# Keys projected from gain-scaled tokens first, their shift added afterwards, and one query projection taken last in the head of a diffusion-transformer block

## The chip, the core and the metric

The kernel runs on one core of one Trainium2 chip. The metric is the device time of one execution in microseconds (us). TensorE (PE) multiplies; ScalarE (ACT) and VectorE (DVE) read its sums from PSUM, convert weights and scale tokens; GpSimd (POOL) and SyncE (SP) issue transfers, ACT some too. Every engine runs its own instructions strictly in order and waits on semaphores.

## What is computed

One block of a diffusion transformer on 256 latent and 256 context tokens of width 2048. Only its beginning matters here:

```python
mod = jax.nn.silu(c) @ ada_w[i] + ada_b[i]                 # (1, 6 * 2048)
sh1, sc1, g1, sh2, sc2, g2 = jnp.split(mod[:, None, :], 6, axis=-1)
mod_c = jax.nn.silu(c_ctx) @ ada_w[i] + ada_b[i]           # the same weights, for the context
h  = rms_norm(x,   norm1_g[i]) * (1 + sc1)  + sh1          # modulate
hc = rms_norm(ctx, norm1_g[i]) * (1 + csc1) + csh1
proj = h @ w_in[i]                                         # q, k, v of two branches, gates
... hc @ w_in[i][:, :N_QKV]                                # q, k, v of the context
```

Two attention branches, their merge, an output projection and a gated MLP with a convolution follow.

## The kernel before

**Number format.** A float32 weight is split into a rounded part w_hi and a remainder w_lo, activations likewise (hT, part 0 and part 1), and a product is hi·hi + hi·lo + lo·hi. A weight unit is 128 x 1024 numbers (two channel groups of 128 by 512 columns, 512 KB). ACT casts it to w_hi, DVE subtracts to w_lo, four such pairs of slots exist (SPLIT_SLOTS), and `raw` has eight landing slots (SLOTS).

**The head.** The 2048 channels are 16 groups `kc`, in four quarters `q`. The modulation product silu(c) @ ada_w for shift and scale is made on PE from raw float32: one `unit_ada(q, kc)` is four matmuls of 32 weight columns over 256 columns each (the profile has eight records for them), reads one 512 KB unit that holds shift and scale columns side by side, and 16 of them finish shift and gain of a quarter. Then a chain runs through three engines: ACT copies the sums (`read_mod_rows`), PE transposes them (`turn_mod`), DVE adds the bias and makes gain and shift (`modulation1`), ACT multiplies the transposed tokens by gain and adds shift (`modulate`, from `turn_tokens` on PE), DVE splits them into hT (`split_modulated`).

**Keys inside the head.** The first job, the keys' projection (job 0), runs between those units: `head_k(s, t)` makes six matmuls for weight unit s (channel groups 2s, 2s+1) and column tile t, once both groups of hT are ready. The table K_TILES says behind which `unit_ada` each of the 32 tiles stands. Job 1 (queries, `projection(1)`) and job 2 (values) follow.

**Other queues.** SP issues all weight loads in the order of HEAD. ACT issues the small parameter loads and the two 2 MB token loads. POOL loads the other columns of ada_w into `ada_raw`, which the keys' weights used until then; DVE sums those in `ada_steps` from job 1 on, by the table ADA_STEPS. From job 1 on each job is a dense run of matmuls with weights two to eight units ahead.

## Time and profile before

| | us |
|---|---|
| median of 3 runs (1720.74 to 1722.42) | 1720.74 |
| the profiled execution | 1720.02 |
| its span, first to last instruction | 1718.3 |
| PE busy / ACT busy / DVE busy in the span | 1677.8 / 752.6 / 1086.3 |
| key tiles start | 52.13 |
| query job (job 1) starts | 131.87 |
| value job (job 2) starts | 154.06 |

A busy PE is not PE at its peak: matmuls overlap in the records, so of a run of them the distance from start to start counts. PEclk is the clock that PE was granted, as a share of 2.4 GHz: 1.00 is 2.4 GHz, 0.50 is 1.2 GHz, and values between are a stretch with both. The chain that ended last is followed back from the last instruction.

### The profile page before, as it was taken

To read this page: it belongs to the slowest core of one execution; us is meant where nothing else is said; L and a number is where in the kernel's file an instruction comes from. 1 tells how busy PE (TensorE), PEld (TensorE's weight loads), DVE (VectorE), ACT (ScalarE), POOL (GpSimd) and SP (SyncE) were. 2 spreads that over 40 slices of the span, in tenths; PEclk is the share of its full clock that TensorE was granted. 3 is DMA by queue.
4 is the path that set the end of the run, shared out by engine and by line. 5 is a ranking of instruction groups with operands and counts; after the bars stand their busy time and mean duration, and the time that the engine had idled before them with its cause. 6 is when DMAs were issued, how large, how long until landed. Compare 5 with 4: busy or idle time off the path is not lost.

```text
span 1718.3 us, 23725 instructions
## 1 busy us (share of the span) xinstructions
PE 1677.8 (98%) x8768; PEld 1371.5 (80%) x8768; DVE 1086.3 (63%) x1366; ACT 752.6 (44%) x962; POOL 108.6 (6%) x161
## 2 busy tenths in 40 slices
PE   4999999999999999999999999999999999999997
PEld 1568888888888678888888788888888888888886
DVE  1338787768887674554555666666666666655556
ACT  2233321623222664444444555555555555544444
POOL 0002222122121000000000000000000000000000
PEclk7999999999999999999999999999999999999999
DMA  9999888269896128566565566666666665655552
GB/s 353 386 387 347 298 296 297 79 215 328 259 321 200 52 90 271 191 189 191 192 234 195 148 190 190 188 191 188 191 187 191 185 184 188 202 195 194 191 193 83
DMA packets 161813, 371.47 MB, mean 216 GB/s; under 512 B 11671, under 2 KB 12423, under 8 KB 160598
## 3 DMA queue, kind: packets, MB, share of 16 engines
q1 hardware_dynamic: 140240, 291.65, 52.5%
q0 software_dynamic: 20144, 74.22, 12.7%
q10 hardware_dynamic: 1366, 4.74, 0.7%
q8 instruction: 41, 0.67, 0.2%
q14 instruction: 22, 0.18, 0.0%
HBM read 368.36 MB, written 2.21 MB: 216 GB/s over the span
## 4 chain that ended last, share of the span: by engine, by line
PE 94%; DMA 3%; DVE 1%; issue 0%; ACT 0%; SPq 0%; DVEq 0%; POOL 0%; ACTq 0%
PE ps L1885 21%; PE ps L1884 11%; PE ps L1899 10%; PE ps L1901 10%; PE ps L1900 10%; PE ps L2253 5%; PE ps L2252 5%; PE ps L2254 5%; PE ps L1811 4%; PE ps L1813 3%; PE ps L1812 3%; DMA raw<-in_ada_w 3%; PE ps L1882 1%; PE ps L1803 1%; PE ps L1968 1%; PE ps L1950 1%
## 5 line engine op out<-in xcount | busy, mean ns | idle before, releaser
L1147 DVE TENSOR_TENSOR w_lo<-raw,w_hi 128x1024 fp32r<-128x1024 f32 x480 | 584.5, 1223 | 419.7 <-ACT w_hi L680 419.2
L680 ACT CAST w_hi<-raw 128x1024 fp32r<-128x1024 f32 x480 | 503.4, 1050 | 763.3 <-PE ps L1885 271.2
L1885 PE MATMUL ps<-h2T,w_hi 128*128 128x512 f32 x1320 | 462.7, 394 | 0.0
L1884 PE MATMUL ps<-h2T,w_lo 128*128 128x256 f32 x1320 | 366.8, 278 | 0.0
L1885 PEld LDWEIGHTS ps<-h2T,w_hi 128*128 128x128 f32 x1320 | 247.8, 188 | 53.7
L1884 PEld LDWEIGHTS ps<-h2T,w_lo 128*128 128x128 f32 x1320 | 248.2, 188 | 3.9
L1899 PE MATMUL ps<-w_hi,hT 128*128 128x512 f32 x512 | 201.7, 394 | 0.0
L1901 PE MATMUL ps<-w_hi,hT 128*128 128x512 f32 x512 | 199.4, 389 | 0.0
L1900 PE MATMUL ps<-w_lo,hT 128*128 128x512 f32 x512 | 199.3, 389 | 0.0
L1222 DVE SCALAR_TENSOR_TENSOR ada_acc<-ada_raw,silu_c,ada_acc 128x512 f32<-128x512 f32 x240 | 179.9, 750 | 29.4 <-DMA ada_raw<-in_ada_w 14.1
L603 POOL DMA_DIRECT2D ada_raw<-in_ada_w x128 | 91.2, 712 | 381.5 <-DVE ada_acc L1222 226.4
L1899 PEld LDWEIGHTS ps<-w_hi,hT 128*128 128x128 f32 x512 | 96.1, 188 | 21.2 <-issue 1.9
L1901 PEld LDWEIGHTS ps<-w_hi,hT 128*128 128x128 f32 x512 | 96.1, 188 | 20.3
L2252 PE MATMUL ps<-w_hi,f_hi 128*128 128x512 f32 x288 | 112.0, 389 | 0.0
L2253 PE MATMUL ps<-w_lo,f_hi 128*128 128x512 f32 x288 | 112.0, 389 | 0.0
L2254 PE MATMUL ps<-w_hi,f_lo 128*128 128x512 f32 x288 | 112.0, 389 | 0.0
L1900 PEld LDWEIGHTS ps<-w_lo,hT 128*128 128x128 f32 x512 | 96.2, 188 | 19.1
L1811 PE MATMUL ps<-hT,w_hi 128*128 128x512 f32 x256 | 103.9, 406 | 1.0 <-DVE hT L1205 1.0
L1813 PE MATMUL ps<-hT,w_lo 128*128 128x512 f32 x256 | 100.0, 390 | 0.0
L1812 PE MATMUL ps<-hT,w_hi 128*128 128x512 f32 x256 | 99.9, 390 | 0.0
L1885 PE MATMUL ps<-hT,w_hi 128*128 128x512 f32 x240 | 84.2, 393 | 0.0
L1884 PE MATMUL ps<-hT,w_lo 128*128 128x256 f32 x240 | 67.3, 280 | 0.0
(231 smaller groups left out, 1985.6 us busy)
## 6 DMA issues: line engine op xcount, KB each, us to landing
raw<-in_ffn_w_up SPq DMA_DIRECT2D x176, 512.0 KB, 3.8
raw<-in_w_in SPq DMA_DIRECT2D x152, 512.0 KB, 4.8
ada_raw<-in_ada_w POOLq DMA_DIRECT2D x128, 512.0 KB, 5.9
raw<-in_ffn_w_down SPq DMA_DIRECT2D x88, 512.0 KB, 4.3
raw<-in_ada_w SPq DMA_DIRECT2D x64, 512.0 KB, 10.4
raw<-in_w_out SPq DMA_DIRECT2D x32, 512.0 KB, 4.4
raw<-in_w_branch_a SPq DMA_DIRECT2D x16, 512.0 KB, 3.6
raw<-in_w_branch_b SPq DMA_DIRECT2D x16, 512.0 KB, 3.6
```

The costliest lines, as they stand in the source:

```text
L680: act.copy(w_hi[:, s % SPLIT_SLOTS, :], raw[:, s, :]).then_inc(hi_ready[s], 1)
L1147: dve.tensor_tensor(w_lo[:, s % SPLIT_SLOTS, :], raw[:, s, :], w_hi[:, s % SPLIT_SLOTS, :], ALU.subtract).then_inc(lo_ready[s], 1)
L1222: dve.scalar_tensor_tensor(acc, raw_columns, silu_c[:, kc:kc + 1], acc, ALU.mult, ALU.add).then_inc(ada_summed, 1)
L1811: pe.matmul(o, w_hi[:, row4(slot), at], hT[:, :, 0, kc, :], start=(kc == 0), stop=False)
L1884: pe.matmul(ps[:, b + t, 0:SEQ], w_lo[:, row4(s), at], high(kc), start=False, stop=False)
L1885: return pe.matmul(o, w_hi[:, row4(s), at], both(kc), start=False, stop=(kc == KC - 1))
L1899: pe.matmul(ps[:, b, :], hi, w_hi[:, row4(s), at], start=(kc == 0), stop=False)
L1900: pe.matmul(ps[:, b, :], hi, w_lo[:, row4(s), at], start=False, stop=False)
L1901: mm = pe.matmul(ps[:, b, :], lo, w_hi[:, row4(s), at], start=False, stop=(kc == last))
L2252: pe.matmul(ps[:, b, :], hi, w_hi[:, row4(s), at], start=start, stop=False)
L2253: pe.matmul(ps[:, b, :], hi, w_lo[:, row4(s), at], start=False, stop=False)
L2254: return pe.matmul(ps[:, b, :], lo, w_hi[:, row4(s), at], start=False, stop=stop)
```

## The change

Shift and gain are now computed as separate groups of four channel groups each (MOD_GROUPS): gain of quarters 0 and 1, gain and shift of quarters 2 and 3, shift of quarters 0 and 1. A `unit_mod(n, i)` takes two channel groups by 512 columns and is again four matmuls; 8 finish a group. For quarters 0 and 1 (LATE = 8 channel groups) the tokens are only scaled, in place (`scale_tokens`, bias 0), and the keys are projected from that. The shift's part of these keys is a vector per column, made from the four key weight units that stay in `ada_raw` (`fix_products`, `turn_fix`, `read_fix`), and DVE adds it to kT in job 2 (`fix_k`). For the queries ACT and DVE add the shift to hT of these groups (`shift_hi`, `shift_lo`), and `head_q` takes weight units in the order of channel pairs 4 to 7, 0 to 3. The last shift group is computed inside the query job. Tokens are loaded by SP ahead of all weights; POOL's loads start when `fix_products` is done; ADA_STEPS has none in job 1.

```diff
-K_AFTER = (3, 10)
-K_TILES = {(0, 0): (1, 6), (0, 1): (1, 8), (0, 2): (1, 10), (0, 3): (1, 12),
...
+MOD_GROUPS = [("gain", 0), ("gain", 1), ("gain", 2), ("shift", 2), ("gain", 3), ("shift", 3), ("shift", 0),
+              ("shift", 1)]
+GAIN_KNOWN = (1, 2, 4, 6)
+LATE = 8
...
+    units = mod(0, range(6)) + weights(0) + mod(0, (6, 7)) + weights(1) + mod(1) + weights(2, 3)
+    units += mod(2) + mod(3, range(6)) + weights(4) + mod(3, (6, 7)) + weights(5)
+    units += mod(4) + mod(5, range(6)) + weights(6) + mod(5, (6, 7)) + weights(7)
+    return units + mod(6) + weights(8, 9, 10, 11) + mod(7) + weights(12, 13, 14, 15)
...
-ADA_STEPS = {1: 12, 2: 34, 3: 13, 4: 37, 5: 32, 6: 24, 7: 13, 8: 28, 9: 13, 10: 32, 11: 18}
+ADA_STEPS = {2: 36, 3: 13, 4: 35, 5: 28, 6: 28, 7: 13, 8: 34, 9: 15, 10: 36, 11: 18}
...
+            def fix_k():
+
+                dve.wait_ge(mod1_ready, MODS + 1)
+                dve.wait_ge(kv_read, 1)
+                keys = kT[:, 0:TILES, :].rearrange("p a (s n) -> p a s n", s=2)
+                dve.tensor_tensor(keys, keys, k_bias[:].unsqueeze(3).to_broadcast([P, TILES, 2, SEQ]), ALU.add)\
                     .then_inc(mod1_ready, 1)
...
-            for _, q, kc in ADA_UNITS:
-                unit_ada(q, kc)
...
+            for i in range(SLOTS):
+                unit_mod(0, i)
+                if i == SLOTS - 2:
+                    turn_tokens(0)
+            turn_mod(0)
+            turn_tokens(1)
+            pe.wait_ge(vecs_ready, 3)
+            for q in range(QUARTERS - 1):
+                first = (1, 2, 4)[q]
+                for n in range(2 * TILES):
+                    head_k(2 * q + n // TILES, n % TILES)
+                    if n in (0, 1):
+                        turn_tokens(SHARE * q + 2 + n)
+                    if n < 4 or q:
+                        for i in range(2):
+                            unit_mod(first + n // 4, 2 * (n % 4) + i)
+                    if n == 4:
+                        turn_tokens(SHARE * (q + 1))
+                        turn_mod(first)
+                if q:
+                    turn_mod(first + 1)
+                turn_tokens(SHARE * (q + 1) + 1)
...
+            for u in range(SLOTS, 2 * SLOTS):
+                head_q(u)
+                if u in (SLOTS + 2, SLOTS + 3):
+                    for i in range(4):
+                        unit_mod(MODS - 1, 4 * (u - SLOTS - 2) + i)
+                if u == SLOTS + 4:
+                    turn_mod(MODS - 1)
+                if u == SLOTS + 5:
+                    fix_products()
+                if u == SLOTS + 6:
+                    turn_fix()
```

The order on PE before, where the sums of the second quarter are turned: L1803 is unit_ada, L1790 turn_mod, L1779 turn_tokens, L1811 to L1813 a key tile.

```order
L1790 MATMUL ps<-consts,mod_rows 128x98 [waits modulated_ready,mod_rows_ready]
...
L1803 MATMUL ps<-raw,c_pair 32x256 [waits raw_landed1]
...
L1813 MATMUL ps<-hT,w_lo 128x512
L1803 MATMUL ps<-raw,c_pair 32x256 [waits raw_landed2]
...
L1779 MATMUL ps<-consts,tokens 128x128 [waits mod1_ready,modulated_ready]
...
L1803 MATMUL ps<-raw,c_pair 32x256 [waits raw_landed3]
```

Three units and a key tile stood between turn_mod and the tokens that wait for its result.

The order on PE after, at the step from channel groups 4 to 7 to groups 8 to 11: L1933 is unit_mod, L1917 turn_mod, L1902 turn_tokens, L1958 the first matmul of a key tile.

```order
L1933 MATMUL ps<-raw,c_pair 32x256 [waits raw_landed0]
L1933 MATMUL ps<-raw,c_pair 32x256 x3
L1917 MATMUL ps<-consts,mod_rows 128x98 [waits modulated_ready,mod1_ready,mod_rows_ready]
L1917 MATMUL ps<-consts,mod_rows 128x98
L1902 MATMUL ps<-consts,tokens 128x128 [waits mod1_ready,modulated_ready]
L1902 MATMUL ps<-consts,tokens 128x128 x3
L1958 MATMUL ps<-hT,w_hi 128x512 [waits lo_ready4,hT_ready]
```

The last product of a shift group, its transposition, the tokens that wait for its result and the key tile that waits for these tokens now stand in a row. The same rows stand at the step to groups 12 to 15; at the step to groups 4 to 7 only the last two of them do:

```order
L1959 MATMUL ps<-hT,w_hi 128x512
L1960 MATMUL ps<-hT,w_lo 128x512
L1902 MATMUL ps<-consts,tokens 128x128 [waits mod1_ready,modulated_ready]
L1902 MATMUL ps<-consts,tokens 128x128 x3
L1958 MATMUL ps<-hT,w_hi 128x512 [waits lo_ready2,hT_ready]
```

Here turn_mod stands three key tiles earlier, but the tokens of group 5 are turned right ahead of the tile that reads them.

## Rows read from the trace of the kernel before

**Rows 1.** The page: PE's busy time, granted clock in 40 slices, and the last-ending chain.

```profile
PE 1677.8 (98%) x8768; PEld 1371.5 (80%) x8768; DVE 1086.3 (63%) x1366; ACT 752.6 (44%) x962; POOL 108.6 (6%) x161
...
PEclk7999999999999999999999999999999999999999
...
PE 94%; DMA 3%; DVE 1%; issue 0%; ACT 0%; SPq 0%; DVEq 0%; POOL 0%; ACTq 0%
```

**Rows 2.** Stretches: busy per engine (PE, PEld, DVE, ACT, POOL), PEclk, DMA share, GB/s.

```profile
52.13:131.87 79.74, 78.54 (x579) 47.83 (x575) 28.13 (x48) 23.30 (x38) 3.44 (x5) 1.00 1.05 386
131.87:154.06 22.19, 22.19 (x129) 19.40 (x128) 19.75 (x24) 10.15 (x9) 6.49 (x10) 1.00 1.02 342
```

**Rows 3.** PE in time order: start, duration, line, operation, names; in brackets idle before.

```profile
37.51 1.08 PE L1803 MATMUL ps<-raw,c_pair 128*32 128x256 f32 x8 [0.26 <-DMA raw<-in_ada_w]
...
39.57 3.08 PE L1803 MATMUL ps<-raw,c_pair 128*32 128x256 f32 x24
42.58 0.39 PE L1790 MATMUL ps<-consts,mod_rows 98*128 98x98 f32 x2
...
45.64 0.79 PE L1803 MATMUL ps<-raw,c_pair 128*32 128x256 f32 x8 [1.48 <-DMA raw<-in_ada_w]
...
50.07 1.12 PE L1779 MATMUL ps<-consts,tokens 128*128 128x128 f32 x4
...
52.13 0.80 PE L1811 MATMUL ps<-hT,w_hi 128*128 128x512 f32 x1
...
319.83 0.63 PE L1926 MATMUL ps<-consts,scores 128*128 128x128 f32 x4 [1.04 <-ACT v_sb L785]
```

**Rows 4.** ACT in time order, same columns.

```profile
40.72 0.37 ACT L752 COPY mod_rows<-ps 98x256 f32<-98x256 f32 x1 [12.07 <-PE ps L1803]
43.48 1.93 ACT L760 ACTIVATE modulated<-ps,shift,gain 128x256 f32<-128x256 f32 x4 [2.39 <-DVE gain L1198]
...
51.28 1.02 ACT L760 ACTIVATE modulated<-ps,shift,gain 128x256 f32<-128x256 f32 x2 [1.04 <-PE ps L1779]
```

**Rows 5.** DVE in time order, same columns.

```profile
46.05 0.69 DVE L1205 TENSOR_TENSOR hT<-modulated,hT 128x512 fp32r<-128x512 f32 x1
...
52.80 0.69 DVE L1205 TENSOR_TENSOR hT<-modulated,hT 128x512 fp32r<-128x512 f32 x1
```

**Rows 6.** PE alone in stretches of 2 us: busy, PEclk, DMA share, GB/s.

```profile
44.00:46.00 2.00, 0.52 (x10) 1.00 1.05 387
46.00:48.00 2.00, 1.43 (x16) 0.50 1.05 387
...
52.00:54.00 2.00, 2.00 (x10) 0.80 1.08 394
...
972.00:974.00 2.00, 0.63 (x4) 1.00 0.89 260
974.00:976.00 2.00, 1.62 (x7) 0.60 0.02 6
...
980.00:982.00 2.00, 2.00 (x10) 0.69 0.67 160
```

**Rows 7.** PE's groups between 52.1 and 131.8 us: line, form, count, busy, mean ns.

```profile
L1803 PE MATMUL ps<-raw,c_pair 128*32 128x256 f32 x332 | 24.9, 391 | 0.2 <-DMA raw<-in_ada_w 0.2
L1779 PE MATMUL ps<-consts,tokens 128*128 128x128 f32 x48 | 7.6, 282 | 0.0
```

**Rows 8.** PE at one sum of job 2: four narrow float32 matmuls, then the next product.

```profile
165.04 0.43 PE L1872 MATMUL ps<-ada_acc,exp_c 128*32 128x128 f32 x8
165.39 0.50 PE L1899 MATMUL ps<-w_hi,hT 128*128 128x512 f32 x1
```

**Rows 9.** A stretch as in rows 2: token loads beside SP's loads.

```profile
12.00:22.00 10.00, 4.49 (x37) 1.61 (x35) 1.58 (x10) 5.70 (x7) 0.00 (x0) 0.83 1.02 418
```

**Rows 10.** The page: a load group (KB, median us to landing), and DVE's sum step.

```profile
L1222 DVE SCALAR_TENSOR_TENSOR ada_acc<-ada_raw,silu_c,ada_acc 128x512 f32<-128x512 f32 x240 | 179.9, 750 | 29.4 <-DMA ada_raw<-in_ada_w 14.1
...
raw<-in_w_in SPq DMA_DIRECT2D x152, 512.0 KB, 4.8
```

More of the change, by code:

```diff
@@ new lines, in shift_hi @@
+            def shift_hi(kc):
+                act.wait_ge(mod1_ready, MODS - 1 + kc // SHARE)
+                act.wait_ge(hT_ready, KC)
+                act.wait_ge(used[kc // 2], 1)
+                for st in range(2):
+                    ins = act.activation(hT[:, st, 0, kc, :].rearrange("p (t n) -> p t n", t=TOK),
+                                         tokens[:, st * TOK:(st + 1) * TOK, kc * P:(kc + 1) * P], ACT.Identity,
+                                         bias=shift_pair[:, 2 * kc + st:2 * kc + st + 1])
+                ins.then_inc(hT_hi_ready, 1)
@@ new lines, in _ @@
+            scale_tokens(KC - 2)
+            scale_tokens(KC - 1)
+            head_hi(SLOTS)
+            read_mod_rows(MODS - 2)
+            head_hi(SLOTS + 1)
+            read_result(JOB_NA)
+            head_hi(SLOTS + 2)
+            head_hi(SLOTS + 3)
+            for kc in range(SHARE):
+                shift_hi(kc)
+            for u in range(SLOTS + 4, 2 * SLOTS - 1):
+                head_hi(u)
+            read_mod_rows(MODS - 1)
+            head_hi(2 * SLOTS - 1)
+            for kc in range(SHARE, LATE):
+                shift_hi(kc)
@@ new lines, in modulation1, with split_scaled @@
+                dve.wait_ge(mod1_step, steps_before + 1)
+                ins = dve.tensor_tensor(by_piece(into), sums[:, 1, 0:2], by_piece(into), ALU.add)
+                if of == "gain":
+                    ins.then_inc(mod1_step, 1)
+                    dve.wait_ge(mod1_step, steps_before + 2)
+                    ins = dve.scalar_tensor_tensor(into, into, 1.0, spread(V_N1), ALU.add, ALU.mult)
+                ins.then_inc(mod1_ready, 1)
+            def split_scaled(kc):
+                dve.wait_ge(modulated_ready, 2 * kc + 2)
+                both = tokens[:, :, kc * P:(kc + 1) * P].rearrange("p (s t) n -> p s t n", s=2)
+                hi, lo = (hT[:, :, part, kc, :].rearrange("p s (t n) -> p s t n", t=TOK) for part in range(2))
+                dve.tensor_copy(hi, both).then_inc(hT_hi_ready, 1)
+                dve.wait_ge(hT_hi_ready, kc + 1)
+                dve.tensor_tensor(lo, both, hi, ALU.subtract).then_inc(hT_ready, 1)
@@ new lines, in fix_products, with turn_fix @@
+            def fix_products():
+                pe.wait_ge(mod1_ready, MODS)
+                for kc in range(LATE):
+                    pair, r = divmod(kc, 2)
+                    for a, at in enumerate(PIECE_AT):
+                        mm = pe.matmul(ps[at:at + 32, FIX_BANK, 0:P], shift_pair[:, 2 * kc:2 * kc + 32],
+                                       ada_raw[:, pair, r, a * P:(a + 1) * P], start=(kc == 0), stop=(kc == LATE - 1))
+                mm.then_inc(ada1_used, 1)
+            def turn_fix():
+                pe.wait_ge(mod_rows_ready, MODS + 1)
+                rows = PIECE_AT[-1] + 2
+                pe.transpose(ps[:, FIX_TURNED_BANK, 0:rows], mod_rows[:, 0, 0:P], consts[0:rows, 0:rows])\
+                    .then_inc(mod_cols_ready, 1)
@@ L1867, in sum_mod @@
+            for n in range(2 * TILES):
+                head_k(SLOTS - 2 + n // TILES, n % TILES)
+                if n in (0, 1):
+                    turn_tokens(KC - 2 + n)
+                if 3 <= n < 7:
+                    for i in range(2):
+                        unit_mod(MODS - 2, 2 * (n - 3) + i)
+            turn_mod(MODS - 2)
             def sum_mod(g, j):
```

413 lines of the change are left out of this document (241 added, 172 removed), and 5 rows, old and new, of the table K_TILES.

## The prediction, made before the changed kernel had run

> **What bounds the kernel now.** I read the page first, then the stretches of the head, then PE, ACT and DVE in order of time around the first key tile, and last the order of instructions of the changed kernel. The page: PE is busy 1677.8 of 1718.3 us, the last-ending chain is 94% PE and 3% DMA, and only the first of 40 slices has less than the full clock [rows 1]. So DMA can be gained on only in the head. There, until 52.13 PE waits for ada_w: the unit at 37.51 starts 0.26 us after PE fell idle, one unit per 1.35 us of transfer [rows 3]. From 52.13, the first key tile, to 131.87 PE is busy 78.54 of 79.74 us at clock 1.00, and in the query job 22.19 of 22.19 [rows 2]. DMA runs at 386 GB/s in that time, so both are full. Behind 154.06, where the value job starts, I take the kernel as unchanged: the answer is when that job starts.
>
> **Start of the keys.** Before, the last product of quarter 0 is the first unit of the row at 39.57 [rows 3]; its data are the 24th half-megabyte (8 of tokens, 16 of ada_w). After, the first gain group ends with the 17th (8 of tokens, 8 of ada_w, one of weights). 7 x 1.35 = 9.5 us less, so landed at about 38.9 - 9.5 = 29.4 instead of 38.9. Then the product, 1.0, and the chain, measured: ACT's copy starts 0.1 later and takes 0.37, PE's transposition 0.39, and from its end (42.97) to the end of the second split (46.05 + 0.69 = 46.74) 3.8 [rows 3 to 5]. 29.4 + 1.0 + 0.1 + 0.37 + 0.1 + 0.39 + 3.8 = 35.2. The tokens move from ACT's queue to SP's, ahead of all weights. While both queues were loaded the rate was 418 GB/s [rows 9], afterwards 386 [rows 2]; 10 us at the lower rate are 0.32 MB, 0.8 us. Bounds 35.2 and 36.0; I take the middle, **35.6**, 16.5 us before 52.13. By the Trainium skill (DMA: Bandwidth & Descriptors, Issuing engines are not separate DMA queues) issuing on several engines saves only issue time; by that the start is 35.2. This row speaks for more, though other transfers differ too.
>
> **Work behind that start.** This is what the early start has to pay for. Before, 23 ada units and 4 token groups were done by 52.13, in time in which PE waited for DMA anyway; after, only 8 and 2 are done by 35.6. So the stretch of the keys (79.7, less its idle 1.0) gets 7 units more (48 for 41; the other 8 go to the query job), 2 token groups and 3 transpositions of sums. A unit costs 24.9 us over 332 records, eight a unit, so 0.6; a token group 7.6/12 = 0.63 [rows 7]; a transposition 0.3 (0.39 at half clock [rows 3]). 78.7 + 4.2 + 1.3 + 0.9 = 85.1. The query job: 22.2 + 8 x 0.6 + 0.3 + fix_products + 0.2. fix_products are eight sets of four narrow matmuls over 128 columns; the nearest set, job 2's sum, takes 0.35 from its start to the next product [rows 8]: 2.8, bounds 2.0 and 4.8 (eight whole units). Sum 30.3. Together **115.4** us against 101.9 before. With no wait at all the value job would start at 35.6 + 115.4 = 151.0, 3.1 before 154.06. That is all that the change can give.
>
> **New waits.** Of the 32 key tiles, four now stand directly behind a chain. At the steps to groups 8 and to 12, PE computes the last unit of a shift group and then nothing but turn_mod and one token group before the tile that reads the result. From the end of the product, at these durations: 0.1 + 0.37 + 0.1 + 0.3 + 3.8 = 4.7, of which PE works 0.3 + 0.6 = 0.9: **3.7 idle each** (rows as above). Shift has two steps on DVE where shift and gain had three; no difference that I can price. At the step to group 4 turn_mod is early, but group 5's tokens are turned right before. In the trace that piece starts at 50.07, PE ends at 51.19, and DVE's split ends at 52.80 + 0.69 = 53.49 [rows 3 to 5]: **2.4 idle**. Behind PE's waiting key tile stand the next units, so their slots free later and SP falls behind too; the eight slots are full then and cover it. Sum 9.8, bounds 8 and 11. Nothing hides them: PE was full, and each is in PE's own order. The fourth is the start itself, counted above.
>
> **Clock.** Twice in the trace PE idles some 2 us and the clock falls from 2.4 to 1.2 GHz. Busy 0.52 of 2.00 in 44 to 46 (1.48 of it in one piece, before 45.64), then 0.50, and 0.80 in 52 to 54: at half from 46 to 52.8. Busy 0.63 of 2.00 in 972 to 974, then 0.60, and 0.69 in 980 to 982: at half from 974.4 to 981.2 [rows 3, 6]. 6.8 us both times, most of it work. At the start of the keys the clock is half as well, since PE waited for DMA and then for the chain. Of such a period I let 4.8 us fall on work, because these waits are longer and part of the period can lie in them: 2.4 lost. At the start, certain: 2.4. At the three steps, likely, as their idle is longer than in both cases seen: 7.2. Sum **9.6**, bounds 2.4 and 13.6. Before had none of it behind 52.8.
>
> **Smaller parts.** The query weights 12 to 15 are loaded into slots that units of the last shift group free, only after head_q(10). w12 is needed 7.4 us later (four units, one head_q of 2.8, four units); a load takes 4.8 from issue to landing [rows 10], conversion 2.3, so 0.3 late; I take 0.5, bounds 0 and 2. Shift on channels 4 to 7 (ACT, DVE) lies behind head_q(13) and fix_products and fits; 0, bound 2. In job 2 DVE adds 36 sum steps of 0.75 [rows 10] and fix_k, twice the elements of a split of 1.2, so 2.3: 0.5 for PE, bounds 0 and 2. The steps taken from job 1 go to jobs with dense PE and spare DVE time: nothing, in either direction, beyond 1 us. The lambda and exp edits are on engines that wait for tokens: nothing.
>
> **Sum.** 35.6 + 115.4 + 9.8 + 9.6 + 0.5 + 0.5 = 171.4 for the start of the value job against 154.06: +17.3. The profiled execution took 1720.0, so 1737.3; it lies 0.7 under the median, so **1738.0**.
>
> **Rivals.** (1) The waits come but the clock stays up at the three steps. For it: the 1.04 us before 319.83 [rows 3] lie in a slice whose clock is 9 on the page, 90% or more [rows 1]. Against: 2 us did not leave it up. Gives 7.2 less, 1730.8; chance 0.16. (2) PE has room in the head, so that the added units fit between key tiles. PE's weight loads are busy only 47.83 of the 79.74 us [rows 2], and if that is PE's real load, the 15 units moved behind the start (9 us) are absorbed: 1729.0. Against it: key matmuls of 512 columns and units start back to back at full clock, without a wait. Chance 0.08. The Trainium skill (Perfetto Trace Analysis, Identifying the Most-Contended Engine) says that weight-load time, not matmul busy time, tells the headroom of PE; this rival is that rule, and I follow the starts instead. (3) Not slower: PE reaches the steps later than the chains end. Its place is turn_mod at the steps to groups 8 and 12, its condition that ACT and DVE finish there within PE's 0.9 us rather than 4.7, and it decides as soon as the three waits sum to under 1 us; then the clock falls only at the start: 171.4 - 9.8 - 7.2 = 154.4, less up to 1 of the smaller parts, thus 1720 to 1721, at best 1717. The order of PE speaks against it, since the product itself is the last thing ahead. Chance 0.07. (4) Late query weights and starved splits of job 2 at their upper bounds, with fix_products at 4.8: 1.5 + 2 + 1.5 + 2 = +7, 1745. Chance 0.10. That the keys don't start earlier I leave out: nothing stands in their way in the order.
>
> **How the numbers follow.** Forecast 0.59, 1733 to 1743. The range takes in rivals 1, 2 and 4: 1727 to 1745. A measurement of this kernel can tell about 0.2%, 3.4 us. Faster by more needs every wait gone and the work undercounted: 0.04. Within: 0.05. Slower: 0.91.
>
> **What the changed profile would show.** First key tile at 35 to 36 with PEclk 0.50. Idle of 3.7, 3.7 and 2.4 ahead of the first matmul of a key tile, released by DVE's split, and PEclk 0.5 behind each. Query job at about 140, value job from 168 to 173. Wrong if those idles are under 1 us, if the clock stays 1.00 over a wait of 3.7, if key tiles interleaved with units take other than 0.23 us a matmul, or if the time behind the value job's start differs by more than 2 us.

## The result, and the profile after

The changed kernel is slower. It took 1733.55 us in the median of 6 runs (1731.6 to 1736.24), the kernel before 1720.74 (6 runs, 1719.35 to 1722.42); the ratio is 1.0077 with a 95% interval of 1.0066 to 1.0088. The forecast was 1738.0 in a range of 1727 to 1745. The profiled execution took 1733.25 us with a span of 1731.5. Run again beside some of the experiments below, the same kernel gave 1.0083 (1.0069 to 1.0096).

The lines of the page that answer [rows 1]:

```profile
span 1731.5 us, 23966 instructions
...
PE 1677.6 (97%) x8841; PEld 1377.7 (80%) x8841; DVE 1096.5 (63%) x1393; ACT 759.4 (44%) x983; POOL 108.4 (6%) x161
...
PEclk9989999999999999999999999999999999999999
...
PE 90%; DVE 5%; DMA 2%; issue 2%; SPq 1%; ACT 1%; POOL 0%; DVEq 0%; POOLq 0%; ACTq 0%
```

PE is as busy as before, 1677.6 for 1677.8 us, in a span that is 13.2 longer. In the chain that ended last PE has 90% where it had 94, and DVE, which had 1, has 5: PE now stands behind DVE.

Two landmarks split the span: the first key tile, and the first matmul of the value job. Before they lie at 52.13 and 154.06. The stretches that they make:

| | first key tile | value job | between | behind |
|---|---|---|---|---|
| before | 52.13 | 154.06 | 101.9 | 1564.2 |
| after | 37.03 | 162.87 | 125.8 | 1568.6 |
| forecast | 35.6 | 171.4 | 135.8 | 1564.2 |

"Behind" counts from the value job to the end of the span; 1.7 us of each profiled execution lie outside it. The keys start 15.1 us earlier, everything up to the value job takes 23.9 longer, and the rest 4.4 longer. Sum 13.2. Neither landmark lies where I put it: the keys start 1.4 us later, and the value job 8.5 us earlier.

**The start.** PE in order of time after, with start, duration, line, operation, names and the idle time before. L1933 is a unit, L1902 a token group, L1917 turn_mod, L1958 the first matmul of a key tile. The view is that of [rows 3]:

```profile
28.82 1.08 PE L1933 MATMUL ps<-raw,c_pair 128*32 128x256 f32 x8 [1.62 <-DMA raw<-in_ada_w]
29.82 1.11 PE L1902 MATMUL ps<-consts,tokens 128*128 128x128 f32 x4
30.87 1.08 PE L1933 MATMUL ps<-raw,c_pair 128*32 128x256 f32 x8
32.45 0.59 PE L1917 MATMUL ps<-consts,mod_rows 98*128 98x98 f32 x2 [0.49 <-ACT mod_rows L779]
33.69 1.11 PE L1902 MATMUL ps<-consts,tokens 128*128 128x128 f32 x4 [0.66 <-DVE gain L1275]
37.03 0.76 PE L1958 MATMUL ps<-hT,w_hi 128*128 128x512 f32 x1 [2.22 <-issue]
...
39.73 1.05 PE L1902 MATMUL ps<-consts,tokens 128*128 128x128 f32 x4
40.71 1.28 PE L1933 MATMUL ps<-raw,c_pair 128*32 128x256 f32 x16
41.92 0.50 PE L1958 MATMUL ps<-hT,w_hi 128*128 128x512 f32 x1
```

Data of the seventh unit land at 28.8, those of the eighth one transfer of 1.35 later, by my estimate at about 30.2. But PE turns the first tokens between them and reaches the eighth unit at 30.87, with no idle before it.

**The waits.** The same view at the steps to groups 4, 8 and 12:

```profile
59.15 0.50 PE L1958 MATMUL ps<-hT,w_hi 128*128 128x512 f32 x1 [2.17 <-DVE hT L1284]
...
81.89 0.39 PE L1917 MATMUL ps<-consts,mod_rows 98*128 98x98 f32 x2 [0.49 <-ACT mod_rows L779]
82.83 0.63 PE L1902 MATMUL ps<-consts,tokens 128*128 128x128 f32 x4 [0.55 <-DVE shift_pair L1271]
86.04 0.80 PE L1958 MATMUL ps<-hT,w_hi 128*128 128x512 f32 x1 [2.58 <-DVE hT L1284]
...
114.26 0.80 PE L1958 MATMUL ps<-hT,w_hi 128*128 128x512 f32 x1 [2.58 <-DVE hT L1284]
```

At group 8 PE idles 0.49 + 0.55 + 2.58 = 3.62 us, and as much at group 12 (0.49 and 0.55 stand at 110.11 and 111.05); at group 4 it is 2.17. Sum 9.41. The kernel before had 1.20 us of idle in all its keys.

**The clock** in stretches of 2 us (columns: stretch, busy of PE, PEld, DVE, ACT and POOL, PEclk, DMA share, GB/s), the answer to [rows 6]:

```profile
84.00:86.00 2.00, 0.00 (x0) 0.00 (x0) 1.93 (x5) 1.58 (x3) 0.00 (x0) 0.89 1.05 392
86.00:88.00 2.00, 1.96 (x5) 1.58 (x6) 1.12 (x1) 0.00 (x0) 0.00 (x0) 0.50 0.69 255
88.00:90.00 2.00, 2.00 (x19) 1.35 (x21) 0.00 (x0) 0.43 (x1) 0.00 (x0) 0.76 0.75 232
...
114.00:116.00 2.00, 1.74 (x4) 1.46 (x5) 1.34 (x2) 0.00 (x0) 0.00 (x0) 0.50 0.87 319
116.00:118.00 2.00, 2.00 (x8) 1.60 (x8) 0.00 (x0) 0.00 (x0) 0.00 (x0) 0.50 0.81 227
118.00:120.00 2.00, 2.00 (x7) 1.57 (x6) 0.77 (x2) 1.02 (x2) 0.00 (x0) 0.58 0.20 74
```

PE is busy all the time and the granted clock is 0.50, 1.2 GHz: in the first pair of stretches 2 x 0.50 + 2 x 0.24 = 1.5 us are lost, in the other 0.9 + 1.0 + 0.84 = 2.7. Behind the wait at group 4 the clock stayed at 1.00. At the start of the keys PEclk shows nothing, but the distances of PE's starts do: the first key tile takes 2.70 us (37.03 to 39.73) where the one at 59.15 takes 1.50, the token group 0.98 where the one at 60.65 takes 0.53, and the pair of units at 40.71 still 1.21 instead of 1.00. So the half clock lasts to about 41.1, and 1.9 are lost. Sum 6.1. By the same distances the other two falls cost 1.3 and 2.5, so PEclk prices them a little too high.

**Job 2.** What PE waited for behind 160 us in more than before; then GpSimd's first four loads, and DVE in order of time in job 2 (L632 is a load of ada_raw, L1943 fix_products, L1319 and L1323 are sum steps, L1217 is a split of weights, L1306 fix_k):

```profile
PE ps L2050 <- DVE w_lo L1217: 3.3, 2, 1.7
...
PE ps L2033 <- DVE w_lo L1217: 1.0, 1, 1.0
```

```profile
157.48 2.87 POOL L632 DMA_DIRECT2D ada_raw<-in_ada_w  x4 [149.06 <-PE ps L1943]
...
165.33 0.49 DVE L1319 TENSOR_SCALAR ada_acc<-ada_raw,silu_c 128x512 f32<-128x512 f32 x1 [3.77 <-DMA ada_raw<-in_ada_w]
...
168.89 1.22 DVE L1217 TENSOR_TENSOR w_lo<-raw,w_hi 128x1024 fp32r<-128x1024 f32 x1
170.03 2.28 DVE L1306 TENSOR_TENSOR kT<-kT,k_bias 128x2048 f32<-128x2048 f32 x1
172.23 4.17 DVE L1323 SCALAR_TENSOR_TENSOR ada_acc<-ada_raw,silu_c,ada_acc 128x512 f32<-128x512 f32 x5
176.32 1.22 DVE L1217 TENSOR_TENSOR w_lo<-raw,w_hi 128x1024 fp32r<-128x1024 f32 x1
```

The first split of two that PE waits for starts late because DVE stood 3.77 us at a sum step whose data GpSimd had not loaded; its loads start only at 157.48, when fix_products has released the slots of ada_raw. The second is late because fix_k and five sum steps, 6.3 us together, run ahead of it. The third wait, of 1.0 us, stands at the start of job 3. In all, PE is idle for 20.2 us behind the value job's start (1568.6 less 1548.5 busy) where it was for 15.7 (1564.2 less 1548.5): by 4.4 more, and these three waits are 4.3 of it.

### The profile page after: what moved, and what is told of

It is laid out like the page before. It is cut to its first block, busy times and chain, and to the rows that moved or that the text cites. A ratio compares the mean times of both kernels' runs of the same rounds, so it can differ in the third digit from the quotient of the medians.

```text
span 1731.5 us, 23966 instructions
## 1 busy us (share of the span) xinstructions
PE 1677.6 (97%) x8841; PEld 1377.7 (80%) x8841; DVE 1096.5 (63%) x1393; ACT 759.4 (44%) x983; POOL 108.4 (6%) x161
## 4 chain that ended last, share of the span: by engine, by line
PE 90%; DVE 5%; DMA 2%; issue 2%; SPq 1%; ACT 1%; POOL 0%; DVEq 0%; POOLq 0%; ACTq 0%
PE ps L2036 19%; PE ps L2035 10%; PE ps L2050 9%; PE ps L2052 9%; PE ps L2051 9%; PE ps L2446 5%; PE ps L2445 5%; PE ps L2444 5%; PE ps L1958 4%; PE ps L1959 3%; PE ps L1960 3%; PE ps L1933 2%; DVE ada_acc L1323 2%; PE ps L2033 1%; DMA ada_raw<-in_ada_w 1%
## 5 line engine op out<-in xcount | busy, mean ns | idle before, releaser
L707 ACT CAST w_hi<-raw 128x1024 fp32r<-128x1024 f32 x472 | 495.9, 1051 | 761.3 <-PE ps L2052 276.3
L1217 DVE TENSOR_TENSOR w_lo<-raw,w_hi 128x1024 fp32r<-128x1024 f32 x472 | 574.9, 1223 | 400.3 <-ACT w_hi L707 400.1
L1323 DVE SCALAR_TENSOR_TENSOR ada_acc<-ada_raw,silu_c,ada_acc 128x512 f32<-128x512 f32 x240 | 180.0, 750 | 29.3 <-DMA ada_raw<-in_ada_w 12.6
L632 POOL DMA_DIRECT2D ada_raw<-in_ada_w x128 | 91.0, 711 | 402.1 <-DVE ada_acc L1323 218.2
L1958 PE MATMUL ps<-hT,w_hi 128*128 128x512 f32 x256 | 106.0, 414 | 9.6 <-DVE hT L1284 7.3
L1959 PE MATMUL ps<-hT,w_hi 128*128 128x512 f32 x256 | 101.7, 397 | 0.0
L1958 PEld LDWEIGHTS ps<-hT,w_hi 128*128 128x128 f32 x256 | 49.1, 192 | 29.2 <-issue 11.8
L2036 PE MATMUL ps<-hT,w_hi 128*128 128x512 f32 x180 | 63.3, 392 | 0.0
```

Source lines behind the costliest of these rows:

```text
L707: act.copy(w_hi[:, s % SPLIT_SLOTS, :], raw[:, s, :]).then_inc(hi_ready[s], 1)
L1217: dve.tensor_tensor(w_lo[:, s % SPLIT_SLOTS, :], raw[:, s, :], w_hi[:, s % SPLIT_SLOTS, :], ALU.subtract).then_inc(lo_ready[s], 1)
L1323: dve.scalar_tensor_tensor(acc, raw_columns, silu_c[:, kc:kc + 1], acc, ALU.mult, ALU.add).then_inc(ada_summed, 1)
L1958: pe.matmul(o, w_hi[:, row4(slot), at], hT[:, :, 0, kc, :], start=(kc == 0), stop=False)
L2036: return pe.matmul(o, w_hi[:, row4(s), at], both(kc), start=False, stop=(kc == KC - 1))
```

## The experiments

Theory A is that of the prediction: what is lost are waits for chains that nothing covers, and the clock behind them. Rival B: PE would be held by the stream of ada_w in any case, so that covering the waits gains little. Later runs ask about the single terms. The landmarks of all kernels are each from its own profiled execution. The kernel before had 1719.7 in the median beside filled waits, group 5 early, steps covered and sums later, and 1720.0 to 1720.1 beside the others:

| kernel | first key tile | value job | between | behind | median | ratio to before (95%) |
|---|---|---|---|---|---|---|
| changed, again | 37.05 | 165.48 | 128.4 | 1566.0 | 1734.59 | 1.0083 (1.0069 to 1.0096) |
| filled waits | 37.94 | 161.01 | 123.1 | 1566.7 | 1729.36 | 1.0054 (1.0040 to 1.0067) |
| group 5 early | 36.75 | 161.26 | 124.5 | 1570.1 | 1731.17 | 1.0064 (1.0051 to 1.0078) |
| steps covered | 37.65 | 159.56 | 121.9 | 1568.1 | 1730.15 | 1.0059 (1.0045 to 1.0073) |
| sums later | 36.47 | 165.00 | 128.5 | 1565.2 | 1731.93 | 1.0077 (1.0063 to 1.0091) |
| fix_k later | 36.27 | 164.80 | 128.5 | 1564.0 | 1731.58 | 1.0067 (1.0054 to 1.0081) |
| units ahead | 37.03 | 152.63 | 115.6 | 1567.6 | 1721.21 | 1.0006 (0.9997 to 1.0015) |
| ahead, sums | 36.76 | 152.79 | 116.0 | 1564.1 | 1719.87 | 1.0003 (0.9994 to 1.0012) |
| single units | 37.90 | 167.97 | 130.1 | 1569.6 | 1739.11 | 1.0107 (1.0092 to 1.0121) |
| tokens by ACT | 38.95 | 167.34 | 128.4 | 1565.8 | 1734.44 | 1.0081 (1.0066 to 1.0095) |
| ahead, fix_k | 36.84 | 152.25 | 115.4 | 1567.1 | 1721.11 | 1.0008 (0.9998 to 1.0017) |
| ahead, fix_k, sums | 37.51 | 152.72 | 115.2 | 1563.3 | 1719.31 | 0.9996 (0.9987 to 1.0004) |

**The changed kernel once more**, unedited.

> The changed kernel itself once more, unchanged, beside the kernel before and the three kernels below on one chip, so that they have a common reference. Expected 1733 us, 0.8% above before. In four profiles of variants whose head is the same up to the first key tile, that tile starts between 36.5 and 37.9 us, with the landing of the small parameter rows (17.9 to 19.3). If the head varies so from execution to execution, the first key tile of this profile lies in 36.4 to 38.0 again and the start's excess over my 35.6 is 1 to 2 us and not a fixed cost.

It started its keys at 37.05, as expected; in the twelve profiles with this order up to the first key tile it starts between 36.27 and 37.94. What differed was the stretch between: 128.4 us for 125.8, with the same waits. Its stretches of 2 us behind group 4:

```profile
60.00:62.00 2.00, 2.00 (x5) 1.63 (x6) 0.98 (x1) 0.00 (x0) 0.00 (x0) 0.50 0.03 8
62.00:64.00 2.00, 2.00 (x18) 1.37 (x21) 0.00 (x0) 0.40 (x2) 0.00 (x0) 0.70 0.00 0
```

After an idle of 2.18 us the clock fell here; after the same idle, 2.17, it had stayed up in the first profile. So this one fall comes in some executions only: it came in four profiles with this wait (this one, sums later, fix_k later, tokens by ACT) and not in three others (the first one, filled waits, single units). What decides it is not shown. The falls that come every time differ in length too. By PEclk the four falls of this profile cost 2.8, 1.6, 2.8 and 1.7 us, 9.0 in all, where the first profile lost 6.1. That is the difference between two executions of one kernel.

**Waits filled with work.** At each of groups 8 and 12 PE computes 22 transpositions that nobody reads, in its idle time; nothing that is needed moves.

```diff
+            def fill(n):
+
+                for _ in range(n):
+                    pe.transpose(ps[:, 4, 0:P], ident, ident)
...
                 if q:
+                    fill(3)
                     turn_mod(first + 1)
+                    fill(3)
                 turn_tokens(SHARE * (q + 1) + 1)
+                if q:
+                    fill(16)
```

> The changed kernel with 22 extra 128x128 transpositions of the identity on PE at each of the steps to groups 8 and 12, into an unused bank, where PE idles 0.49, 0.55 and 2.58 us: 3, 3 and 16 of them. Nothing else moves. Theory A (these waits let the clock fall, and that costs time of its own: half speed from 86.0 to about 89 and from 114.3 to 119.7 in the changed kernel, 1.5 and 2.6 us): the first key tile behind each wait runs at 0.23 us a matmul, the query job starts about 4 us earlier than at 133.8, total about 1729.5. Rival B (the clock costs nothing, because what follows waits for transfers anyway): no change, 1733.5. If the fill overruns the waits, up to 0.5 us later per step.

```profile
84.57 1.91 PE L1990 MATMUL ps<-consts 128*128 128x128 f32 x16
87.33 0.50 PE L1958 MATMUL ps<-hT,w_hi 128*128 128x512 f32 x1 [0.85 <-DVE hT L1284]
```

The chain still takes as long (from the tokens at 84.11 to the key tile 3.2 us, as from 82.83 to 86.04), but the first matmul behind it takes 0.50 us instead of 0.80, and the mean granted clock from 52 to 150 us is 1.00, for 0.95 in the first profile of the changed kernel and 0.93 in the second. The median is 1729.36, or 4.2 us under the first median of the changed kernel and 5.2 under the second. The clock is thus a cost of its own that useless work can avoid, and it is worth about what theory A gave it at two steps.

**Group 5's tokens behind the sixth key tile** instead of behind the eighth, which covers the wait at group 4 alone.

```diff
+                    if n == 5 and q == 0:
+                        turn_tokens(SHARE + 1)
                 if q:
                     turn_mod(first + 1)
-                turn_tokens(SHARE * (q + 1) + 1)
+                    turn_tokens(SHARE * (q + 1) + 1)
```

> The changed kernel with the transposition of group 5's tokens two key tiles earlier, behind the sixth tile of the first block instead of the eighth. Theory A: the wait of 2.17 us ahead of the first tile of groups 4 and 5 goes and nothing takes its place, as PE has weights and units in store: 2.2 us faster, 1731.4. Rival B (transfers hold the head): the 2.2 us come back as waits for ada_w before the query job: 1733.5.

The tile of group 4 follows its predecessor at once. The median is 1731.17, 2.4 us under the changed kernel, for a wait of 2.17, and the forecast was 1731.4. The intervals of the two ratios overlap, so it is the profile and not the median that shows the gain.

**Steps covered.** In quarters 1 and 2 four units follow each of the first four key tiles, so that the sums are known four tiles ahead of the step.

```diff
-                    if n < 4 or q:
-                        for i in range(2):
-                            unit_mod(first + n // 4, 2 * (n % 4) + i)
+                    if n < 4:
+                        for i in range(4 if q else 2):
+                            unit_mod(first + n // 2 if q else first, 4 * (n % 2) + i if q else 2 * n + i)
+                    if n == (2 if q else 4):
+                        turn_mod(first)
                     if n == 4:
                         turn_tokens(SHARE * (q + 1))
-                        turn_mod(first)
-                if q:
-                    turn_mod(first + 1)
-                turn_tokens(SHARE * (q + 1) + 1)
+                        if q:
+                            turn_mod(first + 1)
+                    if n == 5:
+                        turn_tokens(SHARE * (q + 1) + 1)
```

> The changed kernel with PE's order in the blocks changed: in the second and third block four units behind each of the first four key tiles instead of two behind each of eight, both sums turned by the fifth tile, and the next odd group's tokens turned behind the sixth, in all three blocks; so two or more key tiles cover every chain. Same instructions. Theory A: the waits of 2.17, 3.62 and 3.62 us and the two clock falls behind them go: 9.4 + 4.1 = 13.5 less, query job at about 120.5, total 1720. Rival B (with PE faster the stream of ada_w is the bound): PE waits for ada_w show up, the query job starts at 125 or later, total 1724 or more.

All three waits for DVE are gone, and PE waits for something else. Its waits from 38 to 135 us, and the stretch 60 to 80:

```profile
PE ps L1933 <- DMA raw<-in_ada_w: 7.9, 7, 2.1
...
60.00:80.00 20.00, 16.37 (x147) 9.45 (x137) 3.77 (x8) 2.63 (x5) 0.00 (x0) 0.87 1.01 366
```

9.4 us of waits became 7.9 us of others, and behind two of these, of 2.15 and 2.04 us, the clock fell as well (0.50 from 76 to 80 and from 106 to 108). The eight slots hold eight units; sixteen are taken in the time of four tiles, at 1.35 us of transfer each, and in 60 to 80 the DMA share is 1.01. The median is 1730.15, not 1720: with this order rival B is right. It doesn't say that DMA lacks the rate for the keys as a whole: in the changed kernel it moved 0 GB/s from 56 to 60 and 8 from 60 to 62, with full slots that PE didn't empty; SyncE's queue stood there for 11.2 us in one piece, waiting for a unit on PE.

**Units ahead.** That suggested an order that uses this hole. One unit follows each of the tiles 5 to 8 of quarter 0, and two follow every tile of the next two quarters, so that between the last product of a shift group and the first key tile that reads its result two other key tiles stand (the tokens are turned between them). The last four units follow tiles 4 and 5 of the last quarter. The instructions are the same, and the demand never exceeds two units a tile.

```diff
+            ahead = [(n, i) for n in range(1, MODS - 1) for i in range(SLOTS)]
...
-                    if n < 4 or q:
-                        for i in range(2):
-                            unit_mod(first + n // 4, 2 * (n % 4) + i)
+                    if n == (3 if q else 4):
+                        turn_mod(first)
                     if n == 4:
                         turn_tokens(SHARE * (q + 1))
-                        turn_mod(first)
-                if q:
-                    turn_mod(first + 1)
-                turn_tokens(SHARE * (q + 1) + 1)
+                    if n == 5 and q == 0:
+                        turn_tokens(SHARE + 1)
+                    if n == 6 and q:
+                        turn_mod(first + 1)
+                    for i in range(2 if n < 4 or q else 1):
+                        unit_mod(*ahead.pop(0))
+                    if n == 6 and q:
+                        turn_tokens(SHARE * (q + 1) + 1)
...
-                if 3 <= n < 7:
+                if n in (3, 4):
                     for i in range(2):
-                        unit_mod(MODS - 2, 2 * (n - 3) + i)
+                        unit_mod(*ahead.pop(0))
```

> The same instructions as the changed kernel; only PE's order of ada units and transpositions differs. Units run on ahead: one behind each of key tiles 5 to 8 of quarter 0 (where the changed kernel has none and DMA idled 5 us with full slots), two behind every tile from then on, so that each shift group's last product stands two key tiles ahead of the tokens that need it. Demand on DMA never exceeds two units per tile. Theory A (the waits and the clock that they cost are the loss, 9.4 and about 4 us): the idle ahead of the key tiles at groups 4, 8 and 12 sums to under 2 us, no wait for ada_w over 1 us in the keys, clock 1.00 from 45 on; value job 12 us earlier behind the first key tile, 114 us instead of 125.8; 1721. Rival B (DMA-bound in the keys, as with four units a tile, where 7.9 us of waits for ada_w took the place of 9.4): waits for ada_w of 4 us or more, 1728 or more.

Its waits of PE from 38 to 135 us, and two stretches, one in the former hole and one at the step to group 12:

```profile
PE ps L1933 <- DMA raw<-in_ada_w: 2.1, 4, 0.7
...
52.00:60.00 8.00, 8.00 (x58) 4.91 (x61) 3.87 (x8) 2.61 (x5) 0.00 (x0) 1.00 0.88 296
...
112.00:114.00 2.00, 2.00 (x13) 1.66 (x12) 1.12 (x2) 1.19 (x3) 0.00 (x0) 1.00 1.00 367
```

DMA moves 296 GB/s from 52 to 60 where it had moved 132, PE doesn't idle at any step, the clock stays up behind the start of the keys, and the stretch between is 115.6 us. The median is 1721.21 against 1734.59 on the same chip: 13.4 us from nothing but the order. This is the strongest test of theory A, and it met its figure, 1721. Rival B is wrong for this order.

**Single units.** In quarters 1 and 2 the two units of a tile are parted, one of them between the tile's two channel groups.

```diff
             def unit_k(s, slot, t, b, between=lambda: None):
 
                 for i in range(2):
                     mm = products_k(slot, t, b, 2 * s + i, i)
+                    if i == 0:
+                        between()
```

> As the changed kernel, but in quarters 1 and 2 the two ada units behind a key tile are parted: one stands between the tile's two channel groups, the other behind the tile. Same matmuls, same demand on DMA, 16 more switches between key matmuls and units. I had charged 0.6 us for each added unit. In the trace of the changed kernel two units in a row take 1.00 us (16 matmuls, 0.0625 each), and the two switches around them 0.09 and 0.10. Theory A (a unit costs 0.5 and a switch to units and back 0.19, so that 48 units in pairs cost what 41 single ones had): 16 x 0.19 = 3.0 us more in the keys, 1.5 in each of quarters 1 and 2; 1737. Rival D (the 4 us by which I overstated the work lie elsewhere, units cost the same however they stand): no change beyond 0.5 us in either quarter; 1734.

A parted unit in this kernel, between two matmuls of key tiles:

```profile
70.01 0.40 PE L1960 MATMUL ps<-hT,w_lo 128*128 128x512 f32 x1
70.34 0.64 PE L1933 MATMUL ps<-raw,c_pair 128*32 128x256 f32 x8
70.91 0.50 PE L1958 MATMUL ps<-hT,w_hi 128*128 128x512 f32 x1
71.24 0.39 PE L1959 MATMUL ps<-hT,w_hi 128*128 128x512 f32 x1
```

From 70.01 to 71.24 are 1.23 us; without the unit two matmuls take 0.47, so it costs 0.76. The changed kernel has pairs:

```profile
71.66 0.39 PE L1960 MATMUL ps<-hT,w_lo 128*128 128x512 f32 x1
71.98 1.07 PE L1933 MATMUL ps<-raw,c_pair 128*32 128x256 f32 x16
72.98 0.66 PE L1902 MATMUL ps<-consts,tokens 128*128 128x128 f32 x4
73.47 0.33 PE L1917 MATMUL ps<-consts,mod_rows 98*128 98x98 f32 x2
```

A pair takes 1.00, with the two switches (0.09 ahead, 0.10 behind where a key tile follows) 1.19. So a further unit in a row costs 0.43, and each switch to units and back 0.33. Sixteen more switches are 5.3 us by that, worked out from rows of these two kernels. Quarter 1, from its first key tile to its last product, took 24.9 us (59.81 to 84.71) for 22.25 in the changed kernel (59.15 to 81.40), quarter 2 26.4 (89.36 to 115.76) for 23.6 (86.04 to 109.62): 2.65 + 2.8 = 5.5. So rival D falls: where units stand matters. Theory A is right that a switch costs, but its 3.0 was too little by nearly half, since I had left out that a first unit takes 0.57 and a second 0.43. The median rose by 4.5.

**Tokens by ACT.** The two token transfers go back to ACT's queue, behind the parameter rows.

```diff
-            sp.dma_start(tokens[:, 0:TOK, :], x[0].rearrange("(t p) n -> p t n", p=P)).then_inc(tokens_landed, 16)
...
+            act.dma_start(tokens[:, 0:TOK, :], x[0].rearrange("(t p) n -> p t n", p=P)).then_inc(tokens_landed, 16)
```

> The changed kernel with the two token transfers issued by ACT behind the parameter rows again, as in the kernel before; all else is kept. Theory A of the start (moving the tokens to SP's queue costs the keys 0 to 1 us, because two loaded queues run at 418 GB/s and one at 394 in 12 to 22, and because PE's transpositions of the parameter rows start at 18.4 instead of 11.5): parameter rows at about 11.5 again, first key tile at 36.0 to 36.6, half a microsecond to 1 us earlier than 37.0. Rival E (the tokens then share the rate with the units and land at 24 to 25 instead of 15 to 20, so squares, normalization and the transposition of group 0 become the last arrival): first key tile at 38 or later and 1 to 3 us slower than the changed kernel.

```profile
31.75 1.11 PE L1902 MATMUL ps<-consts,tokens 128*128 128x128 f32 x4 [1.83 <-DVE tokens L1358]
32.79 1.08 PE L1933 MATMUL ps<-raw,c_pair 128*32 128x256 f32 x8
...
38.95 0.76 PE L1958 MATMUL ps<-hT,w_hi 128*128 128x512 f32 x1 [2.22 <-issue]
```

Here my theory of the start fell and rival E holds. The parameter rows are turned at 11.94 (11.51 in the kernel before, 18.39 in the changed one), but the seventh unit starts at 28.83, so its data land no earlier than they did (28.82), and now PE waits 1.83 us for normalized tokens. The keys start 1.9 us later. The median shows no difference (1.0081 against 1.0083), so 1.9 us of start are not resolved there.

**Sum steps later, fix_k later.** Two edits for job 2: six sum steps go to jobs 4 and 5 and none stand in job 2's first two slots; or fix_k moves to job 3.

```diff
-ADA_STEPS = {2: 36, 3: 13, 4: 35, 5: 28, 6: 28, 7: 13, 8: 34, 9: 15, 10: 36, 11: 18}
-ADA_SPAN = {JOB_DIFF - 1: range(6), JOB_DIFF: range(3, SLOTS), JOB_MERGE - 1: range(4)}
+ADA_STEPS = {2: 30, 3: 13, 4: 37, 5: 32, 6: 28, 7: 13, 8: 34, 9: 15, 10: 36, 11: 18}
+ADA_SPAN = {JOB_NA + 2: range(2, SLOTS), JOB_DIFF - 1: range(6), JOB_DIFF: range(3, SLOTS), JOB_MERGE - 1: range(4)}
```

> The changed kernel with DVE's sum steps of job 2 only from its third weight unit on, 30 instead of 36, the other 6 in jobs 4 and 5. Theory A (DVE waits 3.8 and 0.7 us for the first ada_w loads of GpSimd with the splits of job 2 queued behind it): both waits of PE for splits in job 2, 1.65 and 1.68, and the 1.0 at the start of job 3 go: 4.3 less, 1729.2. Rival C (the key fix of 2.28 us on DVE is what makes the second split late): only the first goes, 1.7 less, 1731.8.

```diff
-                    if (j, s) == (JOB_NA + 2, 1):
+                    if (j, s) == (JOB_NA + 3, 1):
```

> Only fix_k moves on DVE from job 2 to the second slot of job 3; the 36 sum steps of job 2 stay. The stretch behind the value job's start was 4.4 us longer than before; with six steps fewer in job 2 it shrank by 3.4 of these. Theory A (fix_k's 2.28 us in front of the splits is what starves PE in job 2): the wait of 1.65 us at the fourth slot goes, 1731.0. Rival C (the sums alone, five of them in a row for 4.17 us): both waits stay at 1.7, or the first comes back as a wait in job 3; within 0.7 us of the changed kernel.

With the sums later, both waits of job 2 are gone, but one of 1.81 comes up in job 3: the first step of the third group now stands there, ahead of a split, and needs a result of PE for which DVE idles 10.4 us. The stretch behind shrank to 1565.2. The forecast, 1729.2, missed: the median is 1731.93, and its ratio is the changed kernel's first one. With fix_k later the second wait of job 2 is gone, and the first stays at 1.42, as its cause, GpSimd's late loads, was not touched; the stretch behind is 1564.0, and the median 3.0 us less on the same chip, for a forecast of 1731.0. The intervals overlap in both cases, so here too the waits in the profile are the evidence. The stretch behind is no clean measure of them: the changed kernel's second profile has 3.2 us of waits in job 2 for 3.3 in the first, yet its stretch is 2.6 shorter, and 1.7 of that is PE's busy time.

**Both terms together**, on the order with units ahead.

> The kernel with the units running ahead, and six sum steps of job 2 moved to jobs 4 and 5, with none in job 2's first two slots. If both terms are independent: 3.4 us less than that kernel, 1717.6, which is 0.1% under before. If the starved splits of job 2 only arise because the value job starts while the ada loads of GpSimd are still late, an earlier value job makes them worse, and the gain of moving the sums differs: 1715 to 1722.

> The kernel with the units running ahead (1721.2), with fix_k on DVE moved from job 2 to job 3. By the theory that the two losses add (PE's waits and clock in the keys; fix_k ahead of the splits in job 2), 3.0 us less, as moving fix_k alone gave: 1718.2, 0.1% under before; the wait of 2.26 us for w_lo at 160.5 goes. If the splits of job 2 are held by the late ada loads of GpSimd instead (DVE waited 4.38 us for one there), that wait stays above 1 us and the time at 1720 to 1721.

> As the kernel with units ahead and fix_k in job 3, and in addition no sum step in the first slot of job 2 and two fewer in the job (one more in each of jobs 4 and 5). If GpSimd's late loads hold DVE at that first slot, this takes the rest of the wait: 1717.5 to 1718. If fix_k was all, no difference to the kernel without it beyond 0.5 us.

Here the terms don't just add. With the sums moved the median is 1719.87, 1.3 under that with units ahead alone, where 3.4 was forecast; one wait of 1.81 stands in job 3 again. With fix_k alone moved it is 1721.11, where 1718.2 was forecast: nothing gained. PE in job 2, first with units ahead alone, then with fix_k moved as well, each with its clock behind the wait (columns: stretch, busy of PE, PEclk, DMA share, GB/s):

```profile
160.53 0.50 PE L2054 MATMUL ps<-w_hi,hT 128*128 128x512 f32 x1 [2.26 <-DVE w_lo L1217]
...
162.00:164.00 2.00, 2.00 (x6) 0.50 0.98 376
```

```profile
159.66 0.50 PE L2054 MATMUL ps<-w_hi,hT 128*128 128x512 f32 x1 [1.78 <-DVE w_lo L1217]
...
162.00:164.00 2.00, 2.00 (x6) 0.52 1.01 378
```

Moving fix_k shortened the wait by 0.48 us only, and the clock fell behind it all the same, which cost 1.7 us in each of the two kernels by PEclk (0.50 and 0.65 in 162 to 166 of the first, 0.63 and 0.52 in 160 to 164 of the second). DVE in job 2 of the second:

```profile
154.76 0.49 DVE L1319 TENSOR_SCALAR ada_acc<-ada_raw,silu_c 128x512 f32<-128x512 f32 x1 [3.86 <-DMA ada_raw<-in_ada_w]
...
158.38 1.22 DVE L1217 TENSOR_TENSOR w_lo<-raw,w_hi 128x1024 fp32r<-128x1024 f32 x1
```

It stands 3.86 us for GpSimd's load, and PE behind it 1.78. With two sum steps fewer in the job and none in its first slot, DVE converts two slots of weights before it waits, PE waits for no split in job 2, and the time is 1719.31, ratio 0.9996 (0.9987 to 1.0004); 1717.5 to 1718 was forecast. That is the lowest median of all kernels and can't be told from the kernel before, nor from units ahead alone, whose interval overlaps.

## Why the prediction was right, and where its terms were off

The direction, the mechanism and the range held: the forecast's own case, not a rival, is what happened. The number was 4.1 us too high against the profiled execution (1737.3 for 1733.25), and that is the sum of larger errors with both signs, 5.3 us too low and 9.4 too high, so part of its closeness is luck. The value job started at 162.87, 8.5 us ahead of my 171.4, and the stretch behind it, which I had left as it was but for 0.5, gave 4.4 of them back:

| term | predicted | measured | difference |
|---|---|---|---|
| start of the keys | 35.6 | 37.0 | +1.4 |
| work of the keys stretch | 85.1 | 96.8 - 9.4 - 6.1 = 81.3 | -3.8 |
| new waits | 9.8 | 9.4 | -0.4 |
| clock | 9.6 | 6.1 | -3.5 |
| query job | 30.3 | 29.1 | -1.2 |
| late query weights | 0.5 | 0 | -0.5 |
| job 2 and what follows | 0.5 | 4.4 | +3.9 |

- **Start.** The order of loads was read rightly. Missed was that PE turns the first tokens between the last two units (0.7 us), the eighth unit's data came 0.4 later than my middle by the estimate above, and the chain was 0.4 longer. I had priced 0.4 us for the tokens' change of queue. The seventh unit's data came at 28.82 with the tokens in SP's queue and at 28.83 with them in ACT's. By the Trainium skill (DMA: Bandwidth & Descriptors, Issuing engines are not separate DMA queues) DMAs issued from several engines run on the same 16 DMA engines, and only issue time is saved. This pair of profiles agrees, but weakly: in the other profiles with the tokens in SP's queue the same unit starts anywhere from 28.05 to 29.71, so a term of 0.4 can't be told from nothing.
- **Work.** The term that was mis-sized most is the 0.6 us for each of seven more units. I took an average for the price of one more. By starts a unit more in a row costs 0.43 and a change to units 0.33. Before there were 41 units in 30 runs, 27.5 us by these prices or 0.67 a unit, so the average was not too high; after there are 48 in 24 runs, 28.6. The change added seven units and took away six switches: 1.1 us more, where I charged 4.2. Token groups (0.49 by starts, not 0.63) and transpositions (0.12, not 0.3) give 0.8 more. Together that is 3.9, for a difference of 3.8. The single-unit experiment bears the sum of the two prices out.
- **Waits.** 3.62, 3.62 and 2.17 for 3.7, 3.7 and 2.4. Each chain could be summed from durations of the trace before, because the order showed that nothing would stand beside it. They and the clock behind them are 13.6 us of the first profile (9.4 and 4.2). With units ahead the stretch between shrank by 10.2 and had 2.1 of new waits and a fall at the start that cost 2.7 instead of 1.9, which accounts for 13.1 of them.
- **Clock.** I counted three falls behind the start as likely; in the first profile there were two, of 1.5 and 2.7 us, in the second three. With the start the second profile lost 9.0, near my 9.6, at 2.2 a fall; the number was too high for the first profile, because the wait of 2.2 us at group 4 lets the clock fall in some executions only.
- **Query job.** fix_products took 2.1 us of PE's time (154.87 to 157.31, less 0.35 for the product that stands between anyway) where I took 2.8, nearer the lower bound 2.0. Four units in a row took 1.87 and 2.03, not 2.4. No query weight was late in this profile.
- **Job 2** is the term that I had under its bound: I allowed up to 2 us; the waits for splits were 3.3 in job 2 and 1.0 at the start of job 3. The step that failed is the sentence that DVE adds 36 sum steps and fix_k, priced as load over the job. What counts is what stands directly ahead of each split in DVE's order, and a transfer of GpSimd's that I had not followed: the change lets its loads wait for fix_products, and the first sum step stood at 165.33 for that.
- **Signs.** The waits came where I had put them, and key tiles between units ran at 0.23 us a matmul. But the first key tile (37.03) lay behind my 35 to 36, the query job (133.79) and the value job (162.87) ahead of my 140 and 168 to 173, the clock stayed up behind one of the three waits, and the time behind the value job's start differed by 4.4, more than the 2 us that I had named as a sign of being wrong. The account of the stages was thus worse than the total.

The rivals: the clock did not stay up at all steps (1), the waits were not covered (3), and (2), that PE has room since its weight loads are busy only 60% of the keys, is out: with the units ahead PE idles 2.1 us in the keys and still needs 115.6 us, or 110.8 without this idle and the 2.7 us of clock, where the kernel before needed 101.9. The Trainium skill (Perfetto Trace Analysis, Identifying the Most-Contended Engine) judges PE's headroom by its arithmetic rate and its weight-load time; for the weight-load time the trace differs here, as in 60 to 80 of the changed kernel PE's weight loads are busy 12.2 of 20.0 us, while matmuls start back to back, and the units that were parted moved the end of quarter 1 by 2.65 us. The bound that I gave for the gain, 3.1 us for a change without any wait, was not passed by any order: those with units ahead reach the value job at 152.3 to 152.8, 1.3 to 1.8 before 154.06. But it came from work that I had charged 5.0 us too high. With the measured start and work (37.0 + 81.3 + 29.1) it would be 147.4, or 6.7 us before; the clock at the start and new waits took the rest, and whether an order can get more of it is open.

## What to carry to other kernels

When a change trades an early start for work behind it, read in the new order what stands between the last product and the first reader of its result; the durations of the old trace then give the wait, and moving the producer two key tiles ahead cost nothing here, because the loads followed at an even pace. Price inserted work by the distances of starts, as a cost for each switch and one for each further unit, not by the average of the old order. Work added to an engine that looks idle is priced by what it stands ahead of, and by whether its own data have landed.

## What the runs showed of the chip

- The same idle of 2.17 to 2.18 us at group 4 let the clock fall from 2.4 to 1.2 GHz in four profiles and left it up in three. In job 2 it fell behind 2.26 us with units ahead and behind 1.78 with fix_k moved as well, and stayed up behind 2.10, 2.11 and 2.26 in tokens by ACT, group 5 early and steps covered. Behind the 2.58 us at groups 8 and 12 it fell every time; with small transpositions in these waits and at most 0.85 us of idle in one piece it stayed up both times. By PEclk a fall cost 1.5 to 3.0 us of PE's time (the longest behind 83.93 in group 5 early).
- The granted clock of the page doesn't show every slow stretch: between 37 and 52 the first profile gives 1.00, while its matmuls started 0.43 us apart up to 41, which is half speed. The mean clocks of two profiles (0.987 before, 0.995 after) therefore said nothing of which of them had lost more.
- DMA fell to 0 GB/s for 4 us (56 to 60) and to 8 for the next two with all slots full, though its mean from 38 to 135 was 295 GB/s; the even order filled this hole and gained from it.
